# A YOCO encoder trunk in split fp32: the first strip pair of each MLP without Strassen, and the plain quarter of K last in every pair

## The reference

```python
h = h + multiscale_pool_mixer(rms_norm(h, mix_norm[0]), pool_w[0], pool_scale[0])
h = h + sqrelu_mlp(rms_norm(h, mlp_norm[0]), w_mlp_in[0], w_mlp_out[0])      # layer 0
k, v = shared_kv(h, kv_norm, w_kv, cos, sin)
h = h + diff_attention(rms_norm(h, mix_norm[1]), k, v, w_q, lam, subln, w_o, ...)
h = h + sqrelu_mlp(rms_norm(h, mlp_norm[1]), w_mlp_in[1], w_mlp_out[1])      # layer 1
return rms_norm(h, final_norm)

def sqrelu_mlp(h, w_in, w_out):          # h 256x2048, w_in 2048x8192, w_out 8192x2048
    u = jax.nn.relu(h @ w_in)
    return (u * u) @ w_out
```

## Time and profile before

| | us |
|---|---|
| runs of the kernel, median (three: 1918.81 to 1920.89) | 1920.31 |
| the profiled execution, its own time | 1917.87 |
| its span in the profile | 1916.1 |
| PE busy in it | 1819.8 (95%) |
| DVE busy in it | 1485.1 (78%) |
| ACT busy in it | 987.0 (52%) |

### The profile page before, as it was taken

One profiled execution on the slowest core, in us unless ns is written; L12 is line 12 of the kernel. 1 busy time (PEld: TensorE's weight loads), 2 busy tenths in 40 slices (PEclk: granted clock), 3 DMA queues, 4 the chain that ended last, 5 costly groups with the idle time before them and its releaser, 6 DMA issues.

```text
span 1916.1 us, 22863 instructions
## 1 busy us (share of the span) xinstructions
PE 1819.8 (95%) x8137; PEld 1499.6 (78%) x8137; DVE 1485.1 (78%) x1390; ACT 987.0 (52%) x993; POOL 9.3 (0%) x15
## 2 busy tenths in 40 slices
PE   7779999999999999999999999699999999999998
PEld 6658787878787788888888878578778787878786
DVE  6997878787978886755557777997888888788866
ACT  5555455464546453744344546554646454555543
POOL 0000000000000000000000000000000000000000
PEclk9999999999999999999999999899999999999999
DMA  8247364555646474566654445354647474646571
GB/s 313 88 139 255 133 220 154 198 199 173 219 154 225 153 255 136 175 197 198 190 189 154 132 154 176 110 199 160 218 149 242 143 252 151 221 132 220 181 255 70
DMA packets 178485, 348.75 MB, mean 182 GB/s; under 512 B 10642, under 2 KB 10852, under 8 KB 178020
## 3 DMA queue, kind: packets, MB, share of 16 engines
q1 hardware_dynamic: 177696, 345.88, 54.5%
q10 hardware_dynamic: 708, 1.81, 0.2%
HBM read 345.55 MB, written 2.10 MB: 181 GB/s over the span
## 4 chain that ended last, share of the span: by engine, by line
PE 76%; DVE 14%; issue 5%; ACT 4%; DMA 1%; DVEq 0%; POOL 0%; ACTq 0%; SPq 0%; POOLq 0%
PE bank L1329 18%; PE bank L1330 18%; PE bank L1331 18%; PE bank L1305 7%; PE bank L1303 7%; PE bank L1304 7%; DVE w_lo L844 5%; ACT w_hi L515 2%; DVE w_lo L854 1%; DVE u_lo_a L948 1%; DVE arena L861 1%; PE bank L1321 1%; DVE arena L864 1%; ACT u_hi_a L607 0%; DVE arena L866 0%
## 5 line engine op out<-in xcount | busy, mean ns | idle before, releaser
L844 DVE TENSOR_TENSOR w_lo<-arena,w_hi 128x2048 fp32r<-128x2048 f32 x160 | 364.7, 2288 | 85.1 <-ACT w_hi L509 72.0
L844 DVE TENSOR_TENSOR w_lo<-raw,w_hi 128x2048 fp32r<-128x2048 f32 x144 | 327.9, 2287 | 58.3 <-ACT w_hi L509 58.0
L1329 PE MATMUL bank<-w_hi,u_hi_a 128*128 128x512 f32 x896 | 348.7, 389 | 0.0
L1331 PE MATMUL bank<-w_hi,u_lo_a 128*128 128x512 f32 x896 | 348.6, 389 | 0.0
L1330 PE MATMUL bank<-w_lo,u_hi_a 128*128 128x512 f32 x896 | 348.6, 389 | 0.0
L1329 PE MATMUL bank<-w_hi,mix_hi 128*128 128x512 f32 x672 | 278.0, 414 | 68.7 <-DVE w_lo L844 51.6
L509 ACT ACTIVATE w_hi<-arena 128x2048 fp32r<-128x2048 f32 x96 | 183.1, 1915 | 182.4 <-PE bank L1331 101.9
L1330 PE MATMUL bank<-w_lo,mix_hi 128*128 128x512 f32 x672 | 271.8, 405 | 0.0
L1331 PE MATMUL bank<-w_hi,mix_lo 128*128 128x512 f32 x672 | 271.0, 403 | 0.0
L509 ACT ACTIVATE w_hi<-raw 128x2048 fp32r<-128x2048 f32 x112 | 209.3, 1906 | 115.2 <-PE bank L1331 92.2
L1329 PEld LDWEIGHTS bank<-w_hi,mix_hi 128*128 128x128 f32 x672 | 132.2, 197 | 109.5 <-DVE w_lo L844 63.5
(11 more groups left out here) (164 smaller groups left out, 2476.1 us busy)
## 6 DMA issues: line engine op xcount, KB each, us to landing
raw<-in_w_mlp_in SPq DMA_DIRECT2D x128, 512.0 KB, 4.6
arena<-in_w_mlp_in SPq DMA_DIRECT2D x128, 512.0 KB, 4.9
raw<-in_w_mlp_out SPq DMA_DIRECT2D x128, 512.0 KB, 6.7
arena<-in_w_mlp_out SPq DMA_DIRECT2D x128, 512.0 KB, 5.0
raw<-in_w_kv SPq DMA_DIRECT2D x64, 512.0 KB, 4.5
raw<-in_w_q SPq DMA_DIRECT2D x32, 512.0 KB, 4.7
raw<-in_w_o SPq DMA_DIRECT2D x32, 512.0 KB, 4.3
raw<-in_pool_w SPq DMA_DIRECT2D x8, 512.0 KB, 7.4
```

Source lines behind the costliest of these rows:

```text
L844: nc.vector.tensor_tensor(w_lo[:, slot:slot + 2], raw_half[half][:, 2 * cd:2 * cd + 2], w_hi[:, slot:slot + 2].bitcast(F32), ALU.subtract) ...
L1329: nc.tensor.matmul(bank[:], hi, w_hi[:, slot, kk, :], start=begin, stop=False)
L1331: return nc.tensor.matmul(bank[:], lo, w_hi[:, slot, kk, :], start=False, stop=end)
```

## The change

It multiplies all four quarters of pair 0 the plain way (`first_pair`, eight plain lots). Pair 1 is the first with Strassen quarters. In all other pairs the order of quarters is 1, 2, 3, 0. The tiles of quarters 1 to 3 that the plain way needs are MIX_11, MIX_12, MIX_22 and the added MIX_21; `entry_tiles` rounds them block by block. The hidden part of pair 0 goes from PSUM straight into ReLU. The shared sums of a pair (`c_shared`) follow quarter 3 and so stand beside the plain quarter. Buffers, counts and slot parities are moved to suit: pair 0 counts 16 slots in place of 28, `PAD` fills up at a layer's end, and the first KV strip is loaded when the end strip leaves its buffer. In ACT's and DVE's steady order the four L948 stand behind lot 3 of the first quarter in place of ahead of it.

```diff
 SP, in_pair:
-                in_unit(layer, 0, 3, 1, at + 10, at + 12)
+                in_unit(layer, 0, 3, 1, at + 6, at + 8)
                 return
...
+                in_unit(layer, p, 1, 0, at - 6, at - 4)
+                in_unit(layer, p, 2, 1, at - 2, at)
+                in_unit(layer, p, 3, 0, at + 6, at + 8)
+                in_unit(layer, p, 0, 1, at + 14, at + 16)
 SP, out_pair:
-                    free = (at - 10, at - 2, at + 2, at + 6)[g]
+                    free = (at - 6, at - 2, at + 2, at + 6)[g]
 ACT:
+            def entry_tiles(layer, n):
+                scale_turned(layer, n, 0)
+                if n < 2:
+                    round_std(layer, n)
+                scale_turned(layer, n, 1)
+                if n < 2:
+                    round_plain(layer, n, 4 * n + 2, 0, 2)
+                else:
+                    round_plain(layer, n, 4 * n, 2, 4)
...
+                if isinstance(p, int) and p == 0:
+                    source = (B_P2, B_P4, B_P3, B_22)[i][:]
+                    act.wait_ge(pe_done, i_at(layer, 0) + 15 + i // 2)
...
                 if isinstance(p, int) and p == 1:
-                    copy_p1(layer, 0)
-                    mix_hi_lots(at, slot, 0, i_landed(layer, p, 0), sums, (0, 1))
-                    square_relu(layer, 0, 0)
-                    mix_hi_lots(at, slot, 0, i_landed(layer, p, 0), sums, (2, 3))
-                    for i in range(1, 4):
+                    mix_hi_lots(at, slot, 0, i_landed(layer, p, 0), sums, (0, 1, 2))
+                    act.wait_ge(rms_done, 2 * layer + 2)
+                    for i in range(4):
                         square_relu(layer, 0, i)
+                    mix_hi_lots(at, slot, 0, i_landed(layer, p, 0), sums, (3,))
                 else:
                     mix_hi_lots(at, slot, 0, i_landed(layer, p, 0), sums, range(4))
                 round_u(layer, p - 1, False)
                 mix_hi_lots(at + 8, slot, 1, i_landed(layer, p, 1), sums + 4, range(4))
+                mix_hi_lots(at + 16, slot, 0, i_landed(layer, p, 2), sums + 8, range(4))
                 for cd in range(2):
-                    hi_pair(at + 16 + 2 * cd, slot + 2 * cd, 0, cd, i_landed(layer, p, 2))
-                mix_hi_lots(at + 20, (slot + 4) % HALVES, 1, i_landed(layer, p, 3), sums + 8, range(4))
+                    hi_pair(at + 24 + 2 * cd, slot + 2 * cd, 1, cd, i_landed(layer, p, 3))
 DVE, in_pair:
-                mix_lo_lots(at, slot, 0, i_landed(layer, p, 0), sums, (2,))
+                mix_lo_lots(at, slot, 0, i_landed(layer, p, 0), sums, (1, 2))
                 if not second:
                     out_add(layer, p - 2, 3)
+                mix_lo_lots(at, slot, 0, i_landed(layer, p, 0), sums, (3,))
                 u_low(layer, p - 1, False)
-                mix_lo_lots(at, slot, 0, i_landed(layer, p, 0), sums, (3,))
                 mix_lo_lots(at + 8, slot, 1, i_landed(layer, p, 1), sums + 4, range(4))
+                mix_lo_lots(at + 16, slot, 0, i_landed(layer, p, 2), sums + 8, range(4))
                 for cd in range(2):
-                    lo_pair(at + 16 + 2 * cd, slot + 2 * cd, 0, cd)
-                mix_lo_lots(at + 20, (slot + 4) % HALVES, 1, i_landed(layer, p, 3), sums + 8, range(4))
+                    lo_pair(at + 24 + 2 * cd, slot + 2 * cd, 1, cd)
 DVE, out_pair:
                 out_lots(layer, p, 4 * par, (0,))
+                c_shared(layer, p + 1)
+                out_lots(layer, p, 4 * par, (1,))
                 c_11(layer, p + 1)
-                out_lots(layer, p, 4 * par, (1, 2))
+                out_lots(layer, p, 4 * par, (2,))
                 c_rest(layer, p + 1)
 PE:
+            def first_pair(layer):
+                at, hb, k = i_at(layer, 0), H_MLP[layer], 2 * layer
+                col1, col2 = (B_P2, B_P4), (B_P3, B_22)
+                for u in range(4):
+                    for row in range(2):
+                        lot = 2 * u + row
+                        slot = 2 * lot % HALVES
+                        begin, end = (lot == 0, lot == 0), (lot == 7, lot == 7)
+                        pe.wait_ge(plain_ready, 6 * layer + (1, 3, 3, 4, 5, 6, 6, 6)[lot])
...
+                        pe.wait_ge(lo_ready, at + 2 * lot + 2)
+                        plain_block(col1, u, row, slot, begin, end).then_inc(pe_done, 1)
+                        if lot == 0:
+                            pe.wait_ge(h_added, hb)
+                        plain_block(col2, u, row, slot + 1, begin, end).then_inc(pe_done, 1)
+                        if lot == 1:
+                            turn_h(k, 2, hb)
+                        if lot == 2:
+                            turn_h(k, 3, hb)
 PE, in_pair:
                 mix_unit(layer, p, 1, at, slot, True, False)
                 mix_unit(layer, p, 2, at + 8, slot, False, False)
-                std_unit(layer, p, at + 16, slot)
-                mix_unit(layer, p, 3, at + 20, (slot + 4) % HALVES, False, True)
+                mix_unit(layer, p, 3, at + 16, slot, False, True)
+                std_unit(layer, p, at + 24, slot)
```

More of the change, by code:

```diff
@@ L54 @@
 S_POOL = 0
-S_MLP = (1, 61)
-S_KV = 45
+S_MLP = (1, 60)
+S_KV = 44
 S_Q = S_KV + 2 * PAIRS
 S_O = S_Q + PAIRS
[L59 to L66, removed]
+PAD = 4
 LANDED = ((2, 0), (66, 32))
@@ L1339, in mixed @@
                 return last
-            def plain(banks, which, slot, begin, end):
-                for kk in range(2):
-                    hi, lo = std_hi[:, 2 * which + kk, :], std_lo[:, 2 * which + kk, :]
-                    for tb in range(TB):
-                        tok = slice(tb * P, (tb + 1) * P)
-                        last = product(banks[tb], hi[:, tok], lo[:, tok], slot, kk, begin and kk == 0, end[tb] and kk == 1)
-                return last
             def turn_u(layer, p):
@@ new lines, in plain_block @@
+            def plain_block(banks, u, row, slot, begin, end):
+                for kk in range(2):
+                    if u == 0:
+                        hi, lo = std_hi[:, 2 * row + kk, :], std_lo[:, 2 * row + kk, :]
+                        parts = [(hi[:, tb * P:(tb + 1) * P], lo[:, tb * P:(tb + 1) * P]) for tb in range(TB)]
+                    else:
+                        r = 2 * (u - 1) + kk
+                        parts = [(mix_hi[:, 2 * row + tb, r, :], mix_lo[:, 2 * row + tb, r, :]) for tb in range(TB)]
+                    for tb in range(TB):
+                        last = product(banks[tb], parts[tb][0], parts[tb][1], slot, kk, begin[tb] and kk == 0, end[tb] and kk == 1)
+                return last
@@ L1409, in mix_unit @@
-                if fresh and steady:
+                if begin and not steady:
+                    pe.wait_ge(relu_done, 32 * layer + 1)
+                mixed(B_P2, MIX_12, u, (slot + 2) % HALVES, begin, False).then_inc(pe_done, 1)
+                if begin and steady:
                     pe.wait_ge(h_added, p * 4 + (hb - 4))
-                elif fresh:
-                    pe.wait_ge(c_added, 64 * layer + 7)
-                mixed(B_P3, MIX_S4, u, (slot + 3) % HALVES, fresh, end).then_inc(pe_done, 1)
+                elif begin:
+                    pe.wait_ge(relu_done, 32 * layer + 3)
@@ L1414, in mix_unit @@
+                mixed(B_P3, MIX_S4, u, (slot + 3) % HALVES, begin, False).then_inc(pe_done, 1)
                 pe.wait_ge(lo_ready, at + 6)
                 mixed(B_P5, MIX_S1, u, (slot + 4) % HALVES, begin, end).then_inc(pe_done, 1)
-                if fresh and not steady:
+                if begin and not steady:
                     turn_u(layer, 0)
-                if first and begin:
-                    pe.wait_ge(t_taken, 2 * (R_H[2 * layer] + 3) + 2)
-                elif begin:
+                if begin:
```

342 lines of the change are left out of this document (155 added, 187 removed).

## The result

| | before | after |
|---|---|---|
| median of four runs (lowest to highest), us | 1920.32 (1918.81 to 1920.89) | 1934.36 (1931.43 to 1935.41) |
| the profiled execution | 1917.87 | 1934.61 |
| its span | 1916.1 | 1932.8 |

A forecast was written before the change was run, and what follows sets the result against it. PE, busy 95% of the span, sets the time except where it waits, mostly for DVE's low parts. Plain entries -35.3, new order +16.7 and clock falls +16.2 sum to -2.4 us, 1917.9 on the median; range 1906 to 1925.

The forecast's parts named there:

- Part 1: Plain pair 0 at both layers' entries: 16.4 us saved in layer 0, 18.9 in layer 1, together -35.3.
- the earlier start: Layer 0's MLP entry: ACT scales two blocks, not four, so PE starts 0.8 us earlier, at 48.5.
- Part 2: Order 1, 2, 3, 0 in steady pairs: a new stall at P5 of quarter 3, +16.7 us together.
- The clock: Half rate after the new stall, 1.62 us each, in 10 of 14 pairs: +16.2 us.
- the edits at no cost: out_pair's first load, c_11, shared sums, KV strip's earlier load and PAD: all hidden, 0 us.
- The KV strip's earlier load and `PAD`: At the KV strip: both hide behind PE, which does not wait for loads there; no cost.
- out_pair's first load and `c_11`: Around the start of out_pair: the later load leaves 8 us for splitting, c_11 is done 1.9 us early; no cost.
- The slower rival: At P5 of quarter 3 the clock falls each time; 14 falls give +4.1, 1924.4 us; chance 0.13 for 13 or 14.
- The rival in which the entry gives half: At the entries, a wait on DVE's activation sums or the squares replaces the old: +17.6, 1935.5 us; chance 0.08.
- The count of ten of fourteen: Falls expected behind the new stall in 12 steady pairs and both pairs 1, from ten of twelve and two of five stalls.

The follow-up runs named there:

- e4: The changed kernel with pairs 1 to 7 in the old quarter order 1, 2, 0, 3 and the first strip and layer 0 turned by four slots; 1879.02 us.
- e7: The kernel before with only DVE's four L948 moved behind lot 3 of quarter 1; 1906.73 us, ratio 0.9926.
- e9: The changed kernel with unread matmuls, 8 ahead of P5 of quarter 2 (steady pairs) and 12 ahead of P5 of quarter 3 (pairs 1 to 7); 1919.4 us.
- e5: The changed kernel with 12 unread matmuls ahead of P5 of quarter 3 in pairs 1 to 7; 1930.35 us.
- e2: The kernel before, with ACT's rounding into the first KV strip's slots held until PE has left four more end strip slots; 1933.87 us.
- e1: The changed kernel with the first strip and layer 0 turned by four slots, so end strip and KV strip orders agree, and PAD dropped from the wait; 1919.55 us.
- e3: The changed kernel with pairs 1 to 7 again in the old quarter order 1, 2, 0, 3, pair 0 still plain; 1891.96 us.

## Why the prediction was wrong

**Part 1 was right.** Forecast were 95.8 and 94.2 us from the MLP to out_pair 0, with the clock's falls counted elsewhere; 97.5 and 94.6 came, and layer 0's holds one fall of 1.6 behind P5 of pair 1's quarter 3. Only the earlier start was not had: 49.20 in place of 48.5. (The terms as written add up to 94.4 for layer 1, not 94.2.) The saving of 32.3 in the trace has its like in the runs: e4 differs from e7 in little but the plain pair 0 and is 27.7 us faster, 23.0 between executions with the same mean clock (0.987).

**Part 2 was right in mechanism.** Two stalls in each steady pair, 2.2 to 2.5 and 3.0 us by starts, were forecast as 2.1 and 3.1. In the pair shown, P5 of quarter 3 starts 29.0 us into it (28.7 in the next) where 28.56 was forecast. With ten falls behind the new stall at 1.62 taken out, the steady stretches lost 35.1 - 16.2 = 18.9 us; the forecast was 16.7.

**The clock was right.** Eleven falls of fourteen, ten forecast. The price of 1.62 is a little high: 24 matmuls behind a stall without a fall start over 5.58 us in the traces, not 5.54, so a fall costs 1.6; e9 bears it out. The Trainium skill (TensorE: Matmul & The Clock Gate, section HAM oscillation) has a rule by which only an idle gap longer than any stall of these pairs brings the 1.2 GHz level. The traces contradict it again: 0.51 and 0.55 behind the 3.0 us stalls, 0.53 in e5 behind one of 2.01.

**The step that failed** stands under the edits at no cost: "The KV strip's earlier load and `PAD` hide behind PE, which does not wait for loads there." PE does not wait for a load there, that much holds. But `PAD` and the new count of pair 0 change which slots the end strip fills last, and the wait in `split` compares against the KV strip's own order. ACT's rounding, not the load, came late; it took DVE's additions to h and PE's turn of h with it. Forecast 0, measured 14.0 in the trace, 13.9 in e2 and 14.8 in e1. With e1's repair the kernel takes 1919.55, inside the range of 1906 to 1925 and 1.7 from the forecast. That closeness is in part luck: in the traces the terms without the KV strip come to +2.8 us where -2.4 was forecast (33.9 saved at the entries and not 35.3, 18.9 lost in the pairs and not 16.7, eleven falls and not ten).

**The other places.** out_pair's first load and `c_11` cost nothing that the trace shows. The slower rival (1924.4) wanted thirteen or fourteen falls; eleven came. The rival in which the entry gives half had 1935.5, within 1.2 us of the time measured, by chance: the entries gave what was forecast, and the 14 us were lost at a place that no rival named.

**Open.** Why the clock falls behind a stall of 2.0 us (in brackets) in one pair and stays up behind one of 2.4 in another is not settled by these runs, and so neither is how many falls a given change will bring. The count of ten of fourteen was taken from stalls of like length, and length does not carry it: the changed kernel's first stalls, of 2.0 to 2.4 us, brought the clock down in two of the twelve steady pairs, while stalls of 2.0 to 2.3 us did so in all twelve in the profiled executions of e3, e4 and e7.

## What to carry to other kernels

When a change alters how many slots of a ring a stage counts, walk the ring up to the next stage that enters it with a fixed order: a hold of four slots on an in-order queue cost 14 us here, since additions that PE needed stood behind it. Where one engine is slower than the other in one kind of block and faster in another, put the faster kind between; behind three Strassen quarters the debt was paid twice in a pair, and the old order was worth 42 us. Cut a change into its parts before judging it: the plain pair 0 and the moved low parts (e7) are gains, the order and the ring are losses, and together they were a small loss.

## What the runs showed of the hardware that was not expected

- Eight matmuls whose result nobody reads, 1.8 us in a stall of 2.2, brought 20 us (1879.02 to 1859.05), which the 13 falls that they removed account for: mean clock 0.987 without, 0.999 with them.
- A fall of the clock at one stall protects the next, since PE comes 1.6 us later to it. So filling one of two stalls moved the fall to the other and brought 4 us, filling both 15.
- In e5 a stall of 2.01 us was followed by 0.53 and one of 2.37 by 1.00, ninety microseconds apart in the same execution: the length of a stall alone does not decide.
